# Mixture-of-experts steps of 64 + 32 + 32 lanes in place of 64 + 64, with two sets of weight copies and three result tables

## The reference

```python
u = rmsnorm(x, norm_ffn_w) * (1 + sc2) + sh2
s = sigmoid(u @ router_w)                       # choice of 8 per token: groups, bias
y = sum over the token's 8 experts e of  gate[t, e] * (silu(u @ w_gate[e]) * (u @ w_up[e])) @ w_down[e]
y = y + (silu(u @ sh_w_gate) * (u @ sh_w_up)) @ sh_w_down
x = x + gt2 * y                                 # then a last rmsnorm
```

## Time and profile before

| | us |
|---|---|
| median of 3 runs (2800.69 to 2803.92) | 2801.4 |
| the profiled execution | 2804.71 |
| its span, first to last instruction | 2802.9 |

### The profile page before, as it was taken

How to read it: one execution, slowest core, us unless ns; L and a number is a source line. 1 busy time by engine, 2 the same in 40 slices (tenths; PEclk the granted TensorE clock), 3 DMA queues, 4 the chain that set the end, 5 groups by cost and what they waited for, 6 DMA issues and landing times. The chain is left out here.

```text
span 2802.9 us, 37288 instructions
## 1 busy us (share of the span) xinstructions
PE 2630.9 (94%) x12050; PEld 1459.5 (52%) x12051; DVE 1270.0 (45%) x1949; ACT 732.4 (26%) x1209; POOL 800.1 (29%) x922
## 2 busy tenths in 40 slices
PE   7997999998989899999999978999999989999993
PEld 3564888874667556666666646633333323333332
DVE  3333333333747487853111166354444444444446
ACT  3213333333424300001100031223333223332322
POOL 1000221211534100000000002456656555556545
PEclk8998999998999999999999989999999999999995
DMA  6530000011011111210210511389888998998944
GB/s 247 216 117 23 19 16 16 23 46 49 24 43 33 32 34 34 64 45 25 96 45 4 206 38 70 120 309 318 261 257 261 331 345 252 313 312 282 344 113 187
DMA packets 161015, 390.32 MB, mean 139 GB/s; under 512 B 20819, under 2 KB 107935, under 8 KB 133001
## 3 DMA queue, kind: packets, MB, share of 16 engines
q1 hardware_dynamic: 132689, 319.65, 31.4%
q0 software_dynamic: 28224, 69.29, 10.4%
HBM read 337.68 MB, written 70.45 MB: 146 GB/s over the span
## 5 line engine op out<-in xcount | busy, mean ns | idle before, releaser
L2580 PE MATMUL ps<-big 128*64 x1344 | 597.7, 598 | 0.0
L2524 POOL DMA_INDIRECT big<-u_rows,big x336 | 365.8, 1089 | 148.7 <-issue 76.9
L2580 PEld LDWEIGHTS ps<-big 128*64 128x64 f32 x1344 | 177.8, 137 | 351.8 <-issue 351.8
L1760 PE MATMUL ps<-big 128*128 128x352 f32 x1152 | 346.8, 461 | 5.7 <-SPq L1696 5.7
L2595 PE MATMUL ps<-big 128*64 x672 | 303.9, 595 | 2.1 <-DVE big L2737 2.1
L1760 PEld LDWEIGHTS ps<-big 128*128 128x128 f32 x1152 | 219.7, 191 | 129.1 <-SPq L1696 6.1
L849 PE MATMUL ps<-big 128*128 128x352 f32 x576 | 205.5, 463 | 2.0 <-DMA big<-in_w_in 1.9
L1304 PE MATMUL ps<-big 128*128 128x352 f32 x576 | 185.2, 469 | 10.2 <-DVE big L1524 7.6
L2595 PEld LDWEIGHTS ps<-big 128*64 128x64 f32 x672 | 92.3, 138 | 194.0 <-issue 194.0
L1774 PE MATMUL ps<-big 128*128 128x352 f32 x576 | 174.4, 459 | 1.6 <-DVE big L1894 1.6
L2540 POOL DMA_INDIRECT y_rows<-big x84 | 145.9, 1736 | 103.5 <-issue 89.4
(11 more groups left out here) (580 smaller groups left out, 4242.4 us busy)
## 6 DMA issues: line engine op xcount, KB each, us to landing
big<-in_exp_w_gate SPq DMA_DIRECT2D x64, 1024.0 KB
big<-in_exp_w_up SPq DMA_DIRECT2D x64, 1024.0 KB
big<-in_exp_w_down SPq DMA_DIRECT2D x64, 1024.0 KB
big<-in_ada_w SPq DMA_DIRECT2D x24, 1024.0 KB, 8.1
big<-in_w_in SPq DMA_DIRECT2D x48, 512.0 KB, 4.1
y_rows<-pick SPq DMA_DIRECT2D x16, 512.0 KB, 14.2
big<-y_rows SPq DMA_DIRECT2D x16, 512.0 KB, 10.7
big<-in_w_in SPq DMA_DIRECT2D x6, 1024.0 KB, 5.3
```

The source lines that it names most:

```text
L1760: ins = pe.matmul(ps[:, c, 0:CW], ring_g[:, q % 2, j, :], k.hT[:, j, c * CW:(c + 1) * CW], start=(j == 0), stop=(j == KT - 1))
L2524: g.indirect_dma_start(out=x_rows[:, u, x * 256:(x + 1) * 256], out_offset=None, in_=u_quarters, in_offset=bass.IndirectOffsetOnAxis(idx_i ...
L2580: pe.matmul(ps[0:SUB, 2 + u, :].rearrange("p (g f) -> p g f", f=FF), xT[:, u, j, 0:SUB], gate_up[:, j], start=(j == 0), stop=(j == KT - 1))
```

## The change

- Lanes are handed out in quarters of 32. Each expert gets ceil(count / 32) quarters, at least three (LEAST). A step has four: one group of 64 lanes and two of 32, of up to three experts. An expert's first rows fill its 64-lane groups, the rest its groups of 32. NBLK becomes 112 and the ranges 0 to 75 and 76 to 111.
- Each product of up and down is three matmuls, for 64, 32 and 32 lanes, at partitions 0, 64 and 96 of one PSUM bank.
- The second small group needs copies too: third_up and third_down, six tiles. They lie where x was (xT); x is stored to DRAM (x_keep) when route begins and comes back into the ring when the last experts are done.
- ScalarE makes five up copies per step (two units' worth before, now second_up[0] and third_up[0..3]), VectorE three up and four down.
- Three result tables. The shared expert's output is now computed with tokens on the partitions and stored as the rows of the first table: four tiles in route, five at the start of experts (TAIL_ON_ACT = 3 drained by ScalarE, two by VectorE). add_shared goes.
- The finish adds three tables; POOL_D is 576.

The core of the diff; cut are renamed names, the areas in memory and the arithmetic of the ranks in route (about a dozen small VectorE operations more):

```diff
-SUB = P // 2
-NSUB = E_N + (T * TOPK - E_N) // SUB
-NBLK = (-(-NSUB // 2) + 3) // 4 * 4
+HALF, QUAD = P // 2, P // 4
+LEAST = 3
+NBLK = (-(-(LEAST * E_N + (T * TOPK - (2 * QUAD + 1) * TOPK) // QUAD) // 4) + 3) // 4 * 4
...
-RANGES = ((0, NBLK - 16), (NBLK - 16, NBLK))
+RANGES = ((0, 76), (76, NBLK))
...
+            sp.dma_start(k.x_keep, k.xT[:, :, :].rearrange("p a b -> p (a b)")).then_inc(k.x_kept, 16)
             for t in range(NT):
...
+            for t in range(SH_DOWN):
+                sp.wait_ge(q["sh_drained"], t + 5)
+                store_shared(k, sp, t)
...
-            st(v.tensor_scalar(cnt_i[:, :], cnt[:, :], float(SUB - 1), None, ALU.add))
-            st(v.tensor_scalar(sub_i[:, :], cnt_i[:, :], 6, None, ALU.arith_shift_right))
-            st(v.tensor_scalar(nblk[:, :], sub_i[:, :], 1.0, None, ALU.max))
-            st(v.tensor_tensor_scan(bend[:, :], k.ones[:, 0:E_N], nblk[:, :], 0.0, ALU.mult, ALU.add))
...
+            st(v.tensor_scalar(cnt_i[:, :], cnt[:, :], float(QUAD - 1), None, ALU.add))
+            st(v.tensor_scalar(sub_i[:, :], cnt_i[:, :], 5, None, ALU.arith_shift_right))
+            st(v.tensor_scalar(quads[:, :], sub_i[:, :], float(LEAST), None, ALU.max))
+            st(v.tensor_tensor_scan(quads_end[:, :], k.ones[:, 0:E_N], quads[:, :], 0.0, ALU.mult, ALU.add))
...
+TAIL_ON_ACT = 3
+TAIL_BANKS = (5, 0)
...
+def store_shared(k, sp, t):
+
+    n = tokens_of(t)
+    sp.dma_start(k.y_rows[t * P:t * P + n, :], k.shared_rows[t % 2][0:n, :]).then_inc(k.shared_stored[t % 2], 16)
...
+    third_up = [k.xT[:, x, 0:D].rearrange("p (g f) -> p g f", g=2) for x in range(4)]
+    third_down = [k.xT[:, 4 + x, 0:D] for x in range(2)]
...
-            for e in range(1, NW - 1):
-                load(e, e)
-            for e in range(NW - 1):
+            def ready(e):
                 sp.wait_ge(weights_loaded[e], 48)
                 sp.sem_inc(weights_ready, 1)
-            sp.wait_ge(shared_added, 1)
-            load(NW - 1, NW - 1)
...
+            for e in range(1, NW):
+                load(e, e)
+            ready(0)
+            tail(4)
+            tail(5)
+            ready(1)
+            for t in range(6, NT):
+                tail(t)
+            ready(2)
...
+            for x, (lo, hi) in enumerate(((0, SLOT), (SLOT, KT * T))):
+                free = sp.value_load(k.end_tab[0:1, E_N - NW + x:E_N - NW + x + 1], min_val=1, max_val=NBLK)
+                wait_before_addressed(sp, down_done, free, sp_passed)
+                sp.dma_start(k.ring[:, lo:hi], k.x_keep[:, lo:hi]).then_inc(f.x_back, 16)
...
-                        pe.wait_ge(up_by_dve if unit % 2 else up_by_act, 2 * n + (unit // 2 + 1))
-                    pe.matmul(ps[0:SUB, 2 + u, :].rearrange("p (g f) -> p g f", f=FF), xT[:, u, j, 0:SUB], gate_up[:, j],
+                        pe.wait_ge(up_by_act, 5 * n + (unit + 2))
+                        if unit:
+                            pe.wait_ge(up_by_dve, 3 * n + unit)
+                    pe.matmul(out[0:HALF], xT[:, u, j, 0:HALF], gate_up[:, j], start=(j == 0), stop=(j == KT - 1))
+                    pe.matmul(out[HALF:HALF + QUAD], xT[:, u, j, HALF:HALF + QUAD], second_up[unit][:, :, cols],
                               start=(j == 0), stop=(j == KT - 1))
-                    ins = pe.matmul(ps[SUB:P, 2 + u, :].rearrange("p (g f) -> p g f", f=FF), xT[:, u, j, SUB:P],
-                                    second_up[unit][:, :, part * FF:(part + 1) * FF], start=(j == 0), stop=(j == KT - 1))
+                    ins = pe.matmul(out[HALF + QUAD:P], xT[:, u, j, HALF + QUAD:P], third_up[unit][:, :, cols],
+                                    start=(j == 0), stop=(j == KT - 1))
                     if part and j < KT - 1:
...
-                        pe.matmul(ps[0:SUB, 5 + half, :], hidT[:, u, j, 0:SUB], k.ring[:, bass.ds(off + (DOWN + j * D + half * 512), 512)],
+                        pe.matmul(out[0:HALF], hidT[:, u, j, 0:HALF], k.ring[:, bass.ds(off + (DOWN + j * D + half * 512), 512)],
                                   start=(j == 0), stop=(j == 1))
-                        ins = pe.matmul(ps[SUB:P, 5 + half, :], hidT[:, u, j, SUB:P], second_down[j][:, half * 512:half * 512 + 512],
+                        pe.matmul(out[HALF:HALF + QUAD], hidT[:, u, j, HALF:HALF + QUAD], second_down[j][:, cols],
+                                  start=(j == 0), stop=(j == 1))
+                        ins = pe.matmul(out[HALF + QUAD:P], hidT[:, u, j, HALF + QUAD:P], third_down[j][:, cols],
                                         start=(j == 0), stop=(j == 1))
...
+            def copies_up(n):
+                offs = ready_offsets(act, n, act_passed)
+                free_up(n, 0)
+                act.activation(second_up[0], up_columns(offs[0], 0), ACT.Copy).then_inc(up_by_act, 1)
+                for unit in range(3):
+                    if unit:
+                        free_up(n, unit)
+                    act.activation(third_up[unit], up_columns(offs[1], unit), ACT.Copy).then_inc(up_by_act, 1)
+                return offs
+
+            def last_copy_up(n, offs):
+                free_up(n, 3)
+                act.activation(third_up[3], up_columns(offs[1], 3), ACT.Copy).then_inc(up_by_act, 1)
...
+            def drain_tail(t):
+                act.wait_ge(tail_filled, t - SH_DOWN + 1)
+                act.wait_ge(k.shared_stored[t % 2], 16 * (t // 2))
+                bank = TAIL_BANKS[t % 2]
+                act.activation(k.shared_rows[t % 2].rearrange("p (b c) -> p b c", b=2), ps[:, bank:bank + 2, :], ACT.Copy).then_inc(tail_by_act, 1)
...
                 def step(n, u):
-                    second_half_up(n + 1)
+                    offs = copies_up(n + 1)
                     silu(n, u)
+                    last_copy_up(n + 1, offs)
                     copy_y(n - 1, 1 - u)
                     copy_hid(n, u)
...
+            def copies_down(n):
+                offs = offsets_of(v, n)
                 if isinstance(n, int) and n == 0:
-                    wait_before_addressed(v, tail_filled, KT - SH_DOWN, dve_passed)
+                    wait_before_addressed(v, tail_filled, NT - SH_DOWN, dve_passed)
                 else:
                     wait_before_addressed(v, down_done, n, dve_passed)
                 for j in range(2):
-                    ins = v.tensor_copy(second_down[j], k.ring[:, bass.ds(off + (DOWN + j * D), D)])
+                    for off, down in zip(offs, (second_down, third_down)):
+                        ins = v.tensor_copy(down[j], k.ring[:, bass.ds(off + (DOWN + j * D), D)])
                 ins.then_inc(down_by_dve, 1)
...
                 def step(n, u, x, times):
                     if not (isinstance(n, int) and n == first + 1):
-                        second_half_down(n - 1)
+                        copies_down(n - 1)
                     turn_x(n + 1, 1 - u, x, times)
-                    off = ready_second(n + 1)
+                    off = ready_offsets(v, n + 1, dve_passed)[0]
                     second_up_unit(n + 1, off, 1)
+                    second_up_unit(n + 1, off, 2)
                     hidden(n, u)
                     second_up_unit(n + 1, off, 3)
                     copy_y(n - 1, 1 - u)
...
+        sp.dma_start(f.third[t][0:n, :], k.y_rows[2 * T + t * P:2 * T + t * P + n, :]).then_inc(f.loaded[t], 16)
...
+        g.wait_ge(f.loaded[t], 48)
         g.tensor_tensor(r, r, f.second[0:n, t, 0:POOL_D], ALU.add).then_inc(f.pool_summed, 1)
-        g.wait_ge(f.pool_summed, t + 1)
+        g.wait_ge(f.pool_summed, 2 * t + 1)
+        g.tensor_tensor(r, r, f.third[t][0:n, 0:POOL_D], ALU.add).then_inc(f.pool_summed, 1)
+        g.wait_ge(f.pool_summed, 2 * t + 2)
         g.wait_ge(f.rows_ready, 1 if t < 8 else 2)
         g.tensor_tensor(r, r, f.rows_of[0:n, t // 8, 0:POOL_D], ALU.mult).then_inc(f.gated, 1)
...
-POOL_D = 704
+POOL_D = 576
...
         st(v.tensor_tensor(mine, mine, f.second[0:n, t, POOL_D:D], ALU.add))
+        st(v.tensor_tensor(mine, mine, f.third[t][0:n, POOL_D:D], ALU.add))
```

More of the change, by code:

```diff
@@ L2129, in route @@
     prefix, cnt = w.take(NT + 1, E_N), w.take(E_N)
-    nblk, bend, steps_row = w.take(E_N), w.take(E_N), w.take(E_N)
+    quads, quads_end, steps_row = w.take(E_N), w.take(E_N), w.take(E_N)
+    first_end, second_end = w.take(E_N + 1), w.take(E_N + 1)
+    first_at, first_rows, jump = w.take(E_N), w.take(E_N), w.take(E_N)
     place, slots, slot_gate = w.take(NT, E_N), w.take(NT, TOPK), w.take(NT, TOPK)
-    slot_i, blk_i, lane_i = (w.take(NT, TOPK).bitcast(mybir.dt.int32) for _ in range(3))
-    blk, lane = w.take(NT, TOPK), w.take(NT, TOPK)
+    beyond = w.take(NT, E_N)
+    slot_i, blk_i, lane_i, group_i = (w.take(NT, TOPK).bitcast(mybir.dt.int32) for _ in range(4))
+    blk, lane, group = w.take(NT, TOPK), w.take(NT, TOPK), w.take(NT, TOPK)
     iota_i, iota_f = w.take(2 * NBLK).bitcast(mybir.dt.int32), w.take(2 * NBLK)
@@ L2136, in route @@
```

(21 more changed lines are left out.)

241 lines of the change are left out of this document (134 added, 107 removed).

## The result

The changed kernel takes 4707.2 us (median of 4 runs, 4706.5 to 4709.0) against 2802.0 us before (4 runs): 1.68 times as long, 95% interval 1.677 to 1.683. The profiled execution took 4706.5 us, with a span of 4704.8. The forecast was 4660 us, from 4500 to 4850.

A forecast was written before the change was run, and what follows sets the result against it. The prediction took TensorE's instruction stream as the bound, with DMA next. From 2804.7 us it removed the old steps' 936.4, added 112 x 24.25 = 2716 and 9, 22, 21, 6 and 16: 4658, so 4660 us, range 4500 to 4850.

The forecast's parts named there:

- The number of steps: Expert stage: 305 quarters need 77 steps, the first range holds 76, so 112 steps run where 84 ran.
- A step of 24.25 us: TensorE, expert step: 12 products of 1.99 us in two phases plus a 0.37 transposition, instead of 10.83 us.
- The step that rested on no row: TensorE products: 64 columns beside 32 others assumed to wait for each other, as at other size changes; 1.99 us a product.
- The sum: Whole kernel: 2804.7 - 936.4 + 2716 + 9 + 22 + 21 + 6 + 16 = 4658, so 4660 us.
- the weights are 64 x 3 MB either way and the DMA share falls with the longer step: Expert stage, weight loads: the same volume under longer steps, with no term for it in the sum.
- The DMA share: Expert stage: a sign to look for in the changed profile, DMA share near 0.4, against 0.84 before.
- The gap between the ranges: TensorE between steps 76 and 77: drained and refilled by copy, add, branch and gather to transposed rows, +22 us.
- The start: Before the first up: store queued behind nine 1 MB loads, +21 us (0 to 35); route's extra work, +6 (2 to 12).
- The end: Finish: VectorE with 448 columns instead of 320 and one sum more, GpSimd three operations of 576, +16 us (8 to 30).
- Side by side: Rival, TensorE products: the three groups overlap, a step stays at 10.83 us, total 3210 us; chance 0.14.
- a lower clock for the whole stage: Rival, expert stage: waits lower TensorE's clock to 1.2 GHz, a step near 45 us, total near 7000; chance 0.02.
- both rivals with 76 steps: Expert stage, 304 quarters or fewer, second range skipped: drained, about 3765 us, chance 0.01; side by side, 2790, chance 0.02.

The follow-up runs named there:

- the sorted one: Changed kernel with all 64-lane matmuls of an up, and of a down, issued ahead of its 32-lane ones: 4410.6 us, 1.574 times before.
- The store experiment: Changed kernel with 80 and 32 steps and separate up-weight signals; SP stores the shared output's last five tiles between experts' loads, not behind all nine: 3851.4 us.
- The same two signals: Gate and up alone release up copies, all three parts the down copies: changed kernel with 80 and 32 steps 3854.6 us, kernel before 2860.5 us.

## Why the prediction was right, point by point

- **The number of steps** was right: 77 needed by the count of the routing, 112 run. The kernel with ranges of 80 shows it from the other side: 80 are enough.
- **A step of 24.25 us** was measured at 24.19. The step that rested on no row, that 64 columns and 32 others don't overlap, is settled by three kernels: 64 + 32 + 32 in the kernel before takes 24.19, four of 32 take 10.81, and the sorted one 21.50. The Trainium skill has a change of the tiling configuration drain the array (TensorEngine Tiling (Array Packing), section Tiling Modes); these three runs agree, for two column sizes on disjoint columns. The Trainium skill's other rule, by which tiles at distinct places overlap (TensorE: Matmul & The Clock Gate, Part 3, The mechanism), holds here for tiles of one size, as the four starts within 0.01 us show, and not across sizes.
- **The sum** against the profiled execution came to 4658 and was 4706.5, so 48.5 short. One term is more than the whole of it: "the weights are 64 x 3 MB either way and the DMA share falls with the longer step". It stands in the sum at nothing and cost 54.9 us; the step, 0.06 us shorter than forecast, took 112 x 0.06 = 6.8 back. The term costed the loads by their volume and found no wait. The volume was indeed no bound, but the signal for an expert's up weights came with its down part, which is loaded only after a down is finished, and at four places that was too late. A longer step gives no cover to copies that hang on a load which the end of that same step starts. In the kernel before with 64 + 32 + 32 lanes, whose step is as long but has two experts, no wait was left.
- **The DMA share** of the expert stage was forecast near 0.4 and was 0.29. The share before gives that by itself: 0.84 x 936.4 / 2799.6 = 0.28.
- **The gap between the ranges** was forecast at 22 and half of the 9 for the pauses before a last down, 26.5; it was 27.65 over the usual step. TensorE's timeline there:

```profile
3719.32 0.44 PE L2688 MATMUL ps<-ident,big 128*128 128x128 f32 x2
3723.88 1.96 PE L2675 MATMUL ps<-big 128*64 x2 [4.13 <-DVE xT L2844]
...
3751.36 1.96 PE L2658 MATMUL ps<-big 128*64 x2 [16.74 <-DVE big L2799]
...
3771.16 0.44 PE L2688 MATMUL ps<-ident,big 128*128 128x128 f32 x2 [1.19 <-DVE big L2805]
```

  It has 4.1 us of waiting for the four down copies (2.4 before, forecast 3.8 to 5), then 16.7 without anything to do where 22 were forecast, and behind each the passes run at the lower clock, 1.96 us for two where 1.07 is usual (a granted clock of 0.50, the level of 1.2 GHz, from 3723.8 to 3729.5 and from 3751.3 to 3757.0). By the starts, the lower clock costs 5.5 us (the four down products take 10.7 instead of 7.9, the eight up products 18.6 instead of 15.9), and 1.2 us of waiting come before the last transposition. The sum had neither. That the total came so near is luck: the idle times are 5.6 shorter than forecast, and the lower clock makes up for it.
- **The start** was forecast at +21 and +6 for route, 27; it was 29.6, of which SP's first load after route shows 4.7 (1793.79, and 1789.13 before). The store experiment shows that the mechanism was right and incomplete: the second store of the chain is nearly as late as the first.
- **The end** was forecast at +16 beside the longer down; 16.7 came, of which 3.4 are the longer down (73.7 us from there to the end with 64 + 32 + 32 lanes in the kernel before, 70.3 without), 13.3 the finish and its pause. VectorE's sums there, to be held against the earlier trace rows:

```profile
L3013 DVE TENSOR_TENSOR big<-big,xT 128x448 f32<-128x448 f32 x8 | 12.6, 1569 | 0.3
L3015 DVE TENSOR_TENSOR big<-big 128x448 f32<-128x448 f32 x8 | 12.5, 1568 | 0.3
...
L3012 DVE TENSOR_TENSOR big<-big 128x448 f32<-128x448 f32 x8 | 5.2, 651 | 9.3 <-DMA xT<-y_rows 9.3
```

  Three operations of 1.57, 1.57 and 0.65 us, 3.8 a tile, for two of 1.50 and 0.86, 2.4 a tile. The prediction counted two operations of 1.50 where the earlier trace rows has one. Forecast were 2.10 for each of the long ones, by their columns; with 448 columns instead of 320 they took 0.07 more. So the time went into the third operation and hardly into the width, and that 13.3 lies near the 16 is luck in part.
- **The rivals.** Side by side (3210) is excluded by the timeline; a lower clock for the whole stage did not come, 0.98; both rivals with 76 steps fall with the count.

## What to carry to other kernels

In these runs (float32, 512 columns streamed, tiles of 128 rows by 64 or 32 columns) a tile's size acts as a state of TensorE: tiles of one size share it for the price of one, a tile of another size waits for their streams to end. A packing that saves lanes but mixes sizes pays with the overlap itself, here 13.4 us in each step, where at best 4 steps of 84 are saved (with ranges of 80); sorted by size it still pays most of that. And where the length of a stage hangs on data and a threshold, count the data against the threshold before anything else: one quarter over 304 cost 799 us.

## What the runs showed that was not expected

- The 0.13 us for a change of size is the small part: of the 13.4 us a step, sorting gave back 2.7. The rest is lost overlap.
- The same two signals took 54 us off a kernel with steps of 24 us and put 59 us on one with steps of 10.8, where SP then waited 495 us for its own loads.
- In the kernel before, 22.8 us over the usual step lie inside the expert stage, hidden from a view by averages; they vanish when the same kernel has 64 + 32 + 32 lanes and steps of 24.19 us, and stay at 22.1 with four tiles of 32.
